# The opening of a decoder layer: the gain g_mix is multiplied in behind the transposes, block by block, and the first loads are taken by turns

## What is computed

```python
def _rmsnorm(x, g):
    y = xf * lax.rsqrt(jnp.mean(xf * xf, axis=-1, keepdims=True) + EPS) * g
def _layer(x, ...):
    h = _rmsnorm(x, g_mix)          # g_mix: one gain per column of x
    z = h @ w_in                    # 1024 x 7680: [u | v_A | q | k | v | gate_A | gate_B]
    ... gMLP branch, dilated attention branch, merge ...
    x = x + merged @ w_o
    x = x + jnp.square(jax.nn.relu(_rmsnorm(x, g_ffn) @ w_ff1)) @ w_ff2
    x = x + jax.nn.sigmoid(_rmsnorm(x, g_ple) @ w_ple_gate) * (pe @ w_ple_proj)
```

## Time and profile before

| | |
|---|---|
| runs | 1040.79, 1042.96, 1041.4 us; median 1041.4 us |
| span of the profiled execution | 1041.0 us; the profile gives no time of its own beside the span, so the median stands 0.4 us above it |
| mean granted TensorE clock | 0.997 |
| busy | PE 1023.5 us (98%), DVE 774.4, ACT 518.5, POOL 245.6 |
| chain that ended last | PE 66%, DVE 13%, ACT 5%, issue 5%, DMA 5%, POOL 3% |
| first matmul of unit 0, first of unit 3 | 14.14 us, 30.87 us |

### The profile page before, as it was taken

The page is one execution under the profiler, slowest core; times in us unless marked ns, Lnnn a source line. Parts: engine busy times, 40 slices in busy tenths (PEclk is TensorE's granted clock), DMA queues, the critical chain, the costliest instruction groups (busy, mean ns, idle before and its releaser), DMA issues.

```text
span 1041.0 us, 20872 instructions
## 1 busy us (share of the span) xinstructions
PE 1023.5 (98%) x8310; PEld 1008.5 (97%) x8310; DVE 774.4 (74%) x1004; ACT 518.5 (50%) x1253; POOL 245.6 (24%) x381
## 2 busy tenths in 40 slices
PE   9999999999999999999999999999999999999997
PEld 7999999999999999999999989999999999999997
DVE  6679888988899878999674368747856875786553
ACT  6773797658845574352264385414522531453332
POOL 2441233122312003958201211100100100012300
PEclk9999999999999999999999999999999999999999
DMA  6557556776687765776843335655664574573412
GB/s 186 192 178 231 200 177 208 227 242 206 208 256 213 210 218 148 224 218 186 258 142 122 122 122 208 214 183 172 229 209 152 195 247 168 171 252 130 162 54 86
DMA packets 131634, 195.89 MB, mean 188 GB/s; under 512 B 32321, under 2 KB 109473, under 8 KB 129746
## 3 DMA queue, kind: packets, MB, share of 16 engines
q1 hardware_dynamic: 107616, 125.51, 37.9%
q0 software_dynamic: 10560, 63.28, 18.3%
q10 hardware_dynamic: 13362, 5.77, 2.0%
HBM read 185.55 MB, written 62.00 MB: 238 GB/s over the span
## 4 chain that ended last, share of the span: by engine, by line
PE 66%; DVE 13%; ACT 5%; issue 5%; DMA 5%; POOL 3%; SPq 3%; ACTq 0%; DVEq 0%; POOLq 0%
PE gm L1347 26%; PE gm L1603 7%; PE psSO L1603 4%; PE gm L1321 4%; PE gm L1322 3%; PE gm L1323 3%; PE psT L1603 3%; DMA w_raw<-in_w_in 3%; PE psSO L1651 2%; PE psSO L1347 2%; PE psT L1347 2%; PE psT L1651 2%; DVE w_lo L1708 2%; POOL kv L2363 2%; ACT prob L1123 2%
## 5 line engine op out<-in xcount | busy, mean ns | idle before, releaser
L1321 PE MATMUL gm<-w_hi,h_hi 128*128 128x256 f32 x640 | 186.9, 292 | 1.1 <-DVE w_lo L1708 0.9
L1322 PE MATMUL gm<-w_hi,h_lo 128*128 128x256 f32 x640 | 180.8, 282 | 0.0
L1323 PE MATMUL gm<-w_lo,h_hi 128*128 128x256 f32 x640 | 180.1, 281 | 0.0
L1347 PE MATMUL gm<-h_hi,w_hi 128*128 128x272 f32 x624 | 132.7, 294 | 0.4 <-ACT z L852 0.4
L1347 PE MATMUL gm<-h_hi,w_lo 128*128 128x272 f32 x624 | 130.0, 290 | 0.0
L1347 PE MATMUL gm<-h_lo,w_hi 128*128 128x272 f32 x624 | 129.4, 289 | 0.0
L1321 PEld LDWEIGHTS gm<-w_hi,h_hi 128*128 128x128 f32 x640 | 120.8, 189 | 3.1 <-issue 1.7
L1323 PEld LDWEIGHTS gm<-w_lo,h_hi 128*128 128x128 f32 x640 | 121.2, 189 | 0.0
L1322 PEld LDWEIGHTS gm<-w_hi,h_lo 128*128 128x128 f32 x640 | 120.6, 188 | 0.0
L2352 POOL DMA_DIRECT2D out_kvs<-in_cache_kv_w x64 | 35.0, 547 | 345.2 <-PE gm L1347 120.6
L1708 DVE TENSOR_TENSOR w_lo<-w_raw,w_hi 128x1024 fp32r<-128x1024 f32 x76 | 90.5, 1228 | 21.3 <-ACT w_hi L755 20.8
(11 more groups left out here) (378 smaller groups left out, 2662.7 us busy)
## 6 DMA issues: line engine op xcount, KB each, us to landing
out_kvs<-in_cache_kv_w POOLq DMA_DIRECT2D x64, 510.0 KB, 4.7
w_raw<-in_w_in SPq DMA_DIRECT2D x60, 512.0 KB, 6.2
w_raw<-in_w_ff SPq DMA_DIRECT2D x36, 512.0 KB, 5.7
kv<-in_cache_kv_w SPq DMA_DIRECT2D x128, 128.0 KB
kv<-in_cache_kv_w SPq DMA_DIRECT2D x64, 256.0 KB
out_kvs<-in_cache_kv_w POOLq DMA_DIRECT2D x32, 508.0 KB, 5.3
w_more<-in_w_ff SPq DMA_DIRECT2D x26, 512.0 KB, 6.1
kv<-in_cache_kv_w POOLq DMA_DIRECT2D x128, 64.0 KB, 3.3
```

Of the source, the lines that this page charges most:

```text
L1321: nc.tensor.matmul(out, lh, wh, start=k == 0, stop=False)
L1322: nc.tensor.matmul(out, ll, wh, start=False, stop=False)
L1323: last = nc.tensor.matmul(out, lh, wl, start=False, stop=k == KD - 1)
L1347: last = nc.tensor.matmul(pair[:, half, 0:HALF], w, x[:, k0 + k, half * HALF:(half + 1) * HALF], start=first, stop=end)
```

## The change

The gain leaves the scaling of the tiles and is applied after the transposes, where a column of x is a partition, so that it is one scalar per partition and block.

- `g_mix` is loaded by ACT's queue as a column, `gcol[:, 0]` (128 partitions x 8, single elements), behind `ident`, which now goes first. `g_row`, the matmuls L1574, `gx_b` and its copies are gone; PE's filler is `busy(9)` ahead of the transposes of tile 0.
- `scale_tile` multiplies by the root alone. DVE does it for tiles 0 and 1 in two halves with `tensor_scalar`; POOL does it for tiles 2, 3 and 4 with a `tensor_tensor` against the broadcast root (`x_late`).
- `tile_hi` becomes eight activations of 128 x 128 per tile, each with its gain as scale; `tile_lo` eight `scalar_tensor_tensor` of 128 x 128. For tile 0 PE is told after every pair of blocks, and its groups start by single blocks (`first_blocks`); for tiles 1 to 3 the waits stay at four blocks.
- For the sample rows DVE first multiplies the transposed rows by the gain into `xg`, and ACT and DVE go on from there.
- Panel 0's `w_lo` is made in four pieces of 512 columns (`first_lo`).
- SP loads tile 0, first half of panel 0, tile 1, second half, by turns. ACT squares tile 1 after panel 0 and tile 0.
- `X_STEPS` is now keyed by unit and group: tile 1 behind group 7 of unit 0 (it was ahead of unit 0), tile 2 behind group 13 of unit 0, tile 3 behind group 5 of unit 1, tile 4 behind group 11 of unit 1.

```diff
-X_STEPS = {10: (2,), 13: (3,), 14: (4,)}
+X_STEPS = {(0, 7): 1, (0, 13): 2, (1, 5): 3, (1, 11): 4}
@@ SP
             for a in range(2):
                 sp.dma_start(xn[:, a], t["x_prompt"][128 * a:128 * a + 128]).then_inc(x_tile_in[a], 16)
-            load_panel(0)
+                sp.dma_start(w_raw[:, a].rearrange("p (k n) -> p k n", k=4), wview(0, a)).then_inc(w_landed[0][a], 16)
@@ ACT
             def tile_hi(a):
-                for half in range(2):
-                    act.wait_ge(xt_ready, 2 * a + half + 1)
-                    nc.scalar.copy(h_hi[:, 4 * half:4 * half + 4, 128 * a:128 * a + 128],
-                                   x_bank(a, half).rearrange("p (k n) -> p k n", k=4)).then_inc(h_hi_done, 1)
+                if a == 0:
+                    act.wait_ge(gain_in, 16)
+                for k in range(KD):
+                    act.wait_ge(xt_ready, k // 2 + 1 if a == 0 else 2 * a + k // 4 + 3)
+                    last = nc.scalar.activation(h_hi[:, k, 128 * a:128 * a + 128], x_block(a, k), ACT.Copy, scale=gcol[:, 0, k:k + 1])
+                    if k % 4 == 3:
+                        last.then_inc(h_hi_done, 1)
+                    elif a == 0 and k % 4 == 1:
+                        last.then_inc(hi_block, 1)
-            act.dma_start(g_row[:], t["g_mix"].partition_broadcast(1)).then_inc(g_row_in, 16)
             act.dma_start(ident[:], t["c_ident"]).then_inc(ident_in, 16)
+            act.dma_start(gcol[:, 0], t["g_mix"].rearrange("(k p) -> p k", p=128), allow_slow_non_contiguous=True).then_inc(gain_in, 16)
             square_tile(0)
-            square_tile(1)
             first_hi(0)
             tile_hi(0)
             first_hi(1)
+            square_tile(1)
+            square_tile(2)
             tile_hi(1)
-            square_tile(2)
             square_tile(3)
             square_tile(4)
             tile_hi(2)
             tile_hi(3)
-            act.wait_ge(xt_ready, 9)
-            v = psS[:, 0:KD * NS].rearrange("p (k n) -> p k n", k=KD)
+            act.wait_ge(xg_done, 1)
+            v = xg[:]
@@ PE
+            def first_blocks(k):
+                if k % 2 == 0:
+                    pe.wait_ge(w_hi_done, k // 4 + 1)
+                    if k % 4 == 0:
+                        pe.wait_ge(w0_part, k // 4 + 1)
+                    else:
+                        pe.wait_ge(w_lo_done, k // 4 + 1)
+                if k % 4 == 3:
+                    pe.wait_ge(h_lo_done, k // 4 + 1)
+                else:
+                    pe.wait_ge(lo_block, k // 4 * 3 + k % 4 + 1)
             def x_transposes(a):
-                pe.wait_ge(x_scaled, a + 1)
+                if a >= 2:
+                    pe.wait_ge(x_late, a - 1)
             ...
-            busy(4)
-            pe.wait_ge(g_row_in, 16)
-            for half in range(2):
-                nc.tensor.matmul(gm[:, half, :], ones[0:1], g_row[:, 512 * half:512 * half + 512], start=True, stop=True).then_inc(g_spread, 1)
-            busy(7)
+            busy(9)
             pe.wait_ge(ident_in, 16)
             x_transposes(0)
-            busy(2)
-            x_transposes(1)
-            pe.wait_ge(gx_done, 2)
@@ DVE
             def scale_tile(a):
                 dve.wait_ge(x_rstd, a + 1)
-                vec.scalar_tensor_tensor(out=v, in0=v, scalar=st[0:rows, 0, a:a + 1], in1=gx_b[0:rows], op0=ALU.mult,
-                                         op1=ALU.mult).then_inc(x_scaled, 1)
+                for half in range(2):
+                    v = xn[:, a, 512 * half:512 * half + 512]
+                    vec.tensor_scalar(v, v, st[:, 0, a:a + 1], None, ALU.mult).then_inc(x_scaled, 1)
+            def tile_lo(a, k0, k1):
+                for k in range(k0, k1):
+                    if a == 0 and k % 4 < 2:
+                        dve.wait_ge(hi_block, k // 4 + 1)
+                    else:
+                        dve.wait_ge(h_hi_done, 2 * a + k // 4 + 1)
+                    at = (slice(None), k, slice(128 * a, 128 * a + 128))
+                    last = vec.scalar_tensor_tensor(out=h_lo[at], in0=x_block(a, k), scalar=gcol[:, 0, k:k + 1], in1=h_hi[at].bitcast(F32),
+                                                    op0=ALU.mult, op1=ALU.subtract)
+            ...
+            scale_tile(0)
+            first_lo(0, 0)
+            dve.wait_ge(gain_in, 16)
+            tile_lo(0, 0, 2)
+            first_lo(0, 1)
+            tile_lo(0, 2, 6)
+            first_lo(1, 0)
+            tile_lo(0, 6, 8)
+            first_lo(1, 1)
             scale_tile(1)
+            tile_lo(1, 0, KD)
+            tile_lo(2, 0, KD)
+            tile_lo(3, 0, KD)
+            dve.wait_ge(xt_ready, 11)
+            vec.tensor_tensor(xg[:], gm[:, 3, 0:KD * NS].rearrange("p (k n) -> p k n", k=KD), bc(gcol[:, 0], 2, NS), ALU.mult).then_inc(xg_done, 1)
@@ POOL, in the loop over a
                 inverse_root(v).then_inc(x_rstd, 1)
+                if a >= 2:
+                    pool.wait_ge(x_rstd, a + 1)
+                    x = xn[:, a] if a < 4 else xs[:]
+                    gp.tensor_tensor(x, x, v.broadcast_to([v.shape[0], D]), ALU.mult).then_inc(x_late, 1)
```

More of the change, by code:

```diff
@@ L592, in x_bank, with x_block @@
         def x_bank(a, half):
-            if a in (0, 3):
-                return psT[:, half]
             if a == 1:
-                return (psS, psO)[half][:]
-            return gm[:, 2 + half]
+                return gm[:, 2 + half]
+            return psT[:, half] if a == 2 else psSO[:, half]
+        def x_block(a, k):
+            if a == 0:
+                return (psT[:, 0], psT[:, 1], psS, psO)[k // 2][:, 128 * (k % 2):128 * (k % 2) + 128]
+            return x_bank(a, k // 4)[:, 128 * (k % 4):128 * (k % 4) + 128]
         def raw(p, hh):
@@ L1280, in between @@
             def between(u, g, groups):
-                if u == 0 and g in X_STEPS:
-                    for a in X_STEPS[g]:
-                        x_transposes(a)
+                if (u, g) in X_STEPS:
+                    x_transposes(X_STEPS[u, g])
                 if u == U_FF and g == 1:
@@ L1310, in natural_unit @@
                     for k in range(KD):
-                        if u < 2 and k % 4 == 0:
+                        if u == x == 0:
+                            first_blocks(k)
+                        elif u < 2 and k % 4 == 0:
                             pe.wait_ge(h_lo_done, 4 * u + 2 * x + k // 4 + 1)
-                        if sub == 0 and x == 0:
+                        if u and sub == 0 and x == 0:
                             panel_split(p, n, k)
@@ L1401, in x_transposes @@
                     for k in range(KD):
-                        last = nc.tensor.transpose(psS[:, NS * k:NS * k + NS], xs[:, 128 * k:128 * k + 128], ident[0:NS, 0:NS])
+                        last = nc.tensor.transpose(gm[:, 3, NS * k:NS * k + NS], xs[:, 128 * k:128 * k + 128], ident[0:NS, 0:NS])
                     last.then_inc(xt_ready, 1)
                 else:
-                    for half in range(2):
[L1406 to L1409, removed]
+                    if a >= 2:
+                        pe.wait_ge(h_lo_done, a - 1)
+                    for k in range(KD):
+                        if a < 2 and k % 4 == 0:
+                            pe.wait_ge(x_scaled, 2 * a + k // 4 + 1)
+                        last = nc.tensor.transpose(x_block(a, k), xn[:, a, 128 * k:128 * k + 128], ident[:])
+                        if k % (4 if a else 2) == (3 if a else 1):
+                            last.then_inc(xt_ready, 1)
             def transposes(job):
@@ L2017, in tile_lo @@
-            def tile_lo(a):
-                for half in range(2):
[L2020 to L2025, removed]
-            scale_tile(0)
-            scale_tile(1)
-            for half in range(2):
-                tile_half_lo(0, half)
-                half_lo(0, half)
@@ L2031, in _ @@
[L2031 to L2034, removed]
-            tile_lo(2)
-            tile_lo(3)
+                for half in range(2):
+                    v = xn[:, a, 512 * half:512 * half + 512]
[9 more added lines that the diff above has]
+                                                    op0=ALU.mult, op1=ALU.subtract)
+                    if k % 4 == 3:
+                        last.then_inc(h_lo_done, 1)
+                    elif a == 0:
+                        last.then_inc(lo_block, 1)
@@ new lines, in first_lo @@
+            def first_lo(hh, y):
+                cols = slice(hh * 1024 + 512 * y, hh * 1024 + 512 * y + 512)
+                dve.wait_ge(w_hi_done, hh + 1)
+                vec.tensor_tensor(w_lo[:, 0, cols], w_raw[:, hh, 512 * y:512 * y + 512], w_hi[:, 0, cols].bitcast(F32),
+                                  ALU.subtract).then_inc(w_lo_done if y else w0_part, 1)
+            scale_tile(0)
+            first_lo(0, 0)
+            dve.wait_ge(gain_in, 16)
+            tile_lo(0, 0, 2)
+            first_lo(0, 1)
```

20 lines of the change are left out of this document (6 added, 14 removed).

## The result

| | before | changed kernel |
|---|---|---|
| median of 6 runs each | 1042.07 us | 1050.32 us (1048.05 to 1053.89) |
| span of the profiled execution, its time | 1041.0 us, about 1042.8 us (worked out below) | 1051.2 us, 1053.2 us |
| mean granted TensorE clock | 0.997 | 0.991 |
| first matmul of unit 0, of unit 3 | 14.14, 30.87 us | 10.87, 39.76 us |

The account below looks back on a forecast made before the run. PE bounds the kernel from unit 3 on. Unit 0 starts 5.4 us earlier, but three transpose latencies and late tile 4 put unit 3 at 35.5 against 30.87, +4.6; span 1045.6 plus 0.4 gives 1046.0 us, range 1043.0 to 1050.3.

Parts of the forecast that it names:

- The sign: Whole kernel: the change makes it slower, chance 0.81; within 0.2% 0.12, faster 0.07.
- the chain that sets the start of unit 3: Opening: tile 4's transposes, ACT's sample rows, evacuation of unit 0, panel 1's rounding, then `w_lo`; unit 3 at 35.5, +4.6 us.
- the term for the gain column: Opening load: issued near 1.2 us, landing at 5.7, before ACT needs it at 7.6; upper bound 9.0.
- What bounds the kernel: PE from unit 3 to the end, busy 994.8 of 1010.1 us; unit 3's shift passes to the time nearly one for one.
- Unit 0 at 8.7: Opening: unit 0's first matmul comes at 8.7 us, 5.4 us earlier than 14.14.
- that rival: Gain column lands late, at 9.0, holding ACT and DVE 1.4 us: +6.0, 1047.4 us; chance 0.10.
- Prices of the blocks: 128 x 128 blocks of the tiles: ACT 0.37 us each, 0.26 apart; DVE 0.335 each, 0.255 apart.
- Blocks are not cheap: Answers the rival of cheap blocks on ACT and DVE (0.17 and 0.20 apart): +2.4, 1043.8 us; chance 0.16.
- The three waits: PE behind transposes of tiles 1 to 3: ACT's and DVE's block latency; 1.5 us idle at unit 1 and its group 8.
- `x = 0`: Unit 0's first groups: PE at the slow pace, 0.65 us a group, from 8.7 to 14.1 us.
- Tile 4 and panel 1: Opening: tile 4's transposes end at 29.5, 6.6 us later; panel 1's first `w_lo` half at 35.45, unit 3 at 35.5.
- the second rival: PE falls to half speed in the opening's waits: up to +9.4, 1050.8 us; chance 0.17 for 1047.5 and above.

Follow-up runs that it names:

- the repeat of the tiles further ahead: Second measurement of the changed kernel with gain as rows, blockwise PE waits, DVE scaling all tiles, transposes still earlier: 1042.17 us, 1.0002 of the kernel before.
- experiment 3: Changed kernel, but the gain loaded as 8 rows ahead of `ident`, turned by PE and copied by DVE: 1049.33 us, 1.0060 of the kernel before.
- the repeat: Changed kernel measured once more, unaltered, on the same chip as the second filler run: 1048.76 us, 1.0064 of the kernel before.
- Experiment 2: Changed kernel, but PE waits for the low halves of tiles 1 to 3 block by block: 1047.37 us, 1.0050 of the kernel before.
- experiment 4: Changed kernel plus filler matmuls around tile 0's transposes and behind tile 1's, run twice: 1051.89 and 1051.36 us, 1.0097 and 1.0087 of the kernel before.
- experiment 1: Changed kernel, but tiles 2, 3 and 4 transposed earlier (groups 11, 14 of unit 0, 3 of unit 1): 1046.00 us, 1.0033 of the kernel before.
- experiment 6: Kernel before, with only tile 4's transposes moved behind group 11 of unit 1: 1044.67 us, 1.0014 of the kernel before.

## Why the prediction came out as it did

It said 1046.0, between 1043.0 and 1050.3; 1050.32 was measured, just outside. The sign held, and so did the chain that sets the start of unit 3; the term for the gain column failed. The size was too small: +4.6 was forecast, +8.2 measured. (Another 0.7 of the 4.3 us between 1046.0 and 1050.32 is the base: the prediction added to 1041.4, and six runs of before have a median of 1042.07.)

- **What bounds the kernel.** Right in the main. In eight of the twelve medians the shift against before lies within 1.2 us of unit 3's (changed: +8.9 at unit 3 and +8.2 in the median, again +7.2 and +7.1; transposes earlier +3.9 and +4.0; waits by block +5.1 and +5.4). The other four lie 1.7 to 2.6 above it: both with filler, the gain as rows, and the repeat of the tiles further ahead.
- **Unit 0 at 8.7: the step that failed.** It came at 10.87, 2.2 late, and the term is "the gain column lands at 5.7". It landed at 9.6, 8.4 us behind its issue and not 4.4, because its 1024 single elements went side by side with the loads of SP. I had held 9.0 as an upper bound and given that rival 0.10; it was the case, and 0.6 beyond the bound. A part of it was not in the sum at all, and would by its place in the chain have cost 1.0 by itself: tile 0 landed that much later (its root ready at 7.12 and not 6.14), 0.7 of it through the single elements, as experiment 3 shows; where the rest comes from is not shown. I took 4.07 as given though the change moves what shares the engines with it. Experiment 3 takes the single elements away and finds unit 0 at 8.77, though tile 0 still lands 0.3 late.
- **"If it comes so late, little of the earlier start survives"** priced this rival at +6.0, 1.4 above the forecast. 4.6 + 2.2 = 6.8 were due: the chain from unit 0 to unit 3 has no slack. It measures 27.2 us in the repeat, with filler and with the gain as rows (35.95 - 8.77) alike, against 26.8 in the prediction. In the repeat the two agree up to tile 4's transposes (20.2 us behind unit 0), and the 0.4 lie behind them.
- **Prices of the blocks.** Right: eight blocks in 2.17 us on ACT and in 2.16 on DVE, 0.26 apart as taken from the earlier trace rows. Blocks are not cheap. A half of the scaling took 0.48 us and not 0.69, two of them 0.88; here the Trainium skill's rule (VectorE: DVE Perf Modes, "The perf-mode tier table") was nearer, with its estimate of 0.42. It was worth little, since the gain came last anyway.
- **The three waits.** Predicted 1.5 us for unit 1 and for its group 8, measured 1.31 and 1.25; for `x = 1` 2.1 (15.0 to 17.1), measured 2.02. Experiment 2 shortens each by the three blocks that it should.
- **`x = 0`.** The prediction let PE's slow pace set its 5.4 us. The traces at the lower level have 5.0 to 5.4, those at full clock (experiment 4) 5.0, because there the chain to tile 1's scaling ends last. So the pace is worth 0.4 us at most.
- **Tile 4 and panel 1.** Right, and shown by experiments 1 and 6: from the end of tile 4's transposes to unit 3 it takes 6.3 us (39.76 - 33.5), against the 6.0 used.
- **The clock.** Two of the falls that the second rival warned of came in the profiled execution, the first at a cost of 0.2 us at most, the second 1.5 us for six groups. The same wait of 2.02 us led to a fall in two traces and to none in two others, and PE kept busy gained nothing. The Trainium skill (TensorE: Matmul & The Clock Gate, "HAM oscillation") tells of a kernel in which longer waits than these between bursts of matmuls put the engine back at its cold clock every time. The traces here agree only in part: the fall comes behind shorter waits as well, but not every time.
- **The sum.** 4.6 forecast, 2.2 for the later start, 1.5 for the fall, 0.2 by which tile 1 came later in that execution, and 0.4 in the chain make 8.9, the shift of unit 3 in the profiled execution. Without the fall it is 7.2, and the medians of changed kernel and repeat, 8.2 and 7.1, lie around both. Two traces of this kernel don't tell how often the fall comes. The 1.3 us behind unit 3 are smaller than what separates one kernel's repeats (2.6, 3.4 and 3.7 in the table), so they can't be told from chance.
- **Chances.** Slower, held at 0.81, came true. The range was drawn from one rival at a time, and no line of the prediction added two. The late start and the longer chain alone (7.2) give 1049.3 on the median of 1042.07, within the range; one fall more gives 1050.8. The repeat's 1048.76 lies inside, so it is by little that the first median lies outside.

## What to carry to other kernels

Where PE's work is fixed, find the moment from which everything hangs and the chain that feeds it; an earlier first matmul was worth nothing here while transposes stood so close to their use that each tile brought its own latency, and moving them ahead gave back more than anything else. A small load by single elements costs by what it shares the engines with, and it delayed the first large load too (by 0.7 us here): load it as rows and turn it. And when several rivals can come true together, price them together; the range must hold the pair.

## What the runs showed of the hardware

- **Single elements beside large loads.** In the window 5 to 6 us ACT's queue moved 494 packets and SP's 271; from 7.5 to 8 us 148 and 150, one for one. The same 4 KB form took 4.4 us in the earlier trace rows and 8.1 to 9.2 in the opening of six traces of kernels that have it there.
- **Executions far longer than the others.** One execution of experiment 1 had a span of 2002.8 us, with a mean of 457 ns for a matmul that takes 280 in the earlier trace rows; matmuls follow each other about 0.24 us apart, against 0.12 at full clock and 0.21 at the lower level. The eleven others took 1041.6 to 1049.3 us. DVE and ACT were busy no longer than usual, so it is PE that was slow. Its profile gives a clock of 1.00, which doesn't fit. That reading is not safe elsewhere either: in the kernel before it stands at 10 to 12 us too, where the transposes take 0.42 us each and not 0.27 as later. An execution in experiment 6 had a span of 2452.9 us (clock 1.00), more than twice the usual, and one of the kernel before had 1406.9 (clock 0.656). Neither was profiled, and no cause is known. Busy times and the group of that matmul in the page of experiment 1:

```profile
PE 1994.6 (100%) x8297; PEld 1942.7 (97%) x8298; DVE 780.7 (39%) x1028; ACT 528.7 (26%) x1277; POOL 242.8 (12%) x384
...
L1344 PE MATMUL gm<-w_hi,h_hi 128*128 128x256 f32 x640 | 292.4, 457 | 1.2 <-DVE h_lo L2035 1.2
```

- **The rest is not fixed to better than some 3 us.** Identical kernels had 1007.9 and 1011.3 us behind unit 3. Falls of the clock are a part of it. In the changed kernel two stretches behind the opening show the lower clock, here their windows:

```profile
380.00:386.00 6.00, 6.00 (x38) 5.91 (x37) 5.57 (x7) 2.46 (x7) 0.00 (x0) 0.72 0.55 193
522.00:528.00 6.00, 4.95 (x28) 4.99 (x29) 1.16 (x3) 0.43 (x2) 0.00 (x0) 0.72 1.03 378
```

The kernel before had one, at 517; the end of each span, where PE has nothing left to do, shows it too. Leaving that end out, the three traces without such a stretch have 1005.9, 1007.0 and 1008.8 us in the table's "rest", the three with two of them 1010.7 to 1011.7, and the seven with one 1007.8 to 1012.3, so the falls do not explain all. Differences of 2 us in the opening are at the edge of what can be told through that.
